# Banded attention on one core: neighbouring sums and maxima, ScalarE copies that round, and the queries' remainder at the fourth step

## The chip, the cores and the metric

One core of a Trainium2 chip runs one program. The time is the device time of one launch in microseconds, and the kernel before has 2769.32 us as the median of 3 runs (2768.60 to 2769.61). TensorE is written PE, VectorE DVE, ScalarE ACT, GpSimd POOL.

## The reference

The program computes two stacks of two layers over 1024 latent rows of width 1024, with 256 context rows beside them in the first stack. Only one part is touched: the banded attention of the first stack's odd layer (`windowed_gqa`), 16 query heads in 4 groups of 4, head size 64.

```
s_ctx  = q . kc * scale                       # all 256 context keys
s_band = q . kb * scale, -inf outside +-128   # own block of 128 and its two neighbours
p = softmax([s_ctx, s_band, sink])            # sink: one learned score per head, no value
o = p[ctx] @ vc + p[band] @ vb                # blocks: 128 queries at a time
```

## The kernel before, in words

The layer's queries are cut into 16 groups, m = 0 to 15. A group is one block of 128 queries (t = m // 2) and one of two pairs of key heads (gp = m % 2), so 8 query heads. A group walks over its tiles of 128 keys, one a step (k): two context tiles and two or three of the band. Groups 0, 1, 14 and 15 (first and last block) have 4 steps, the other twelve have 5. `gsteps` lists all steps n of all groups, `last_step[m]` is the last one of group m.

Scores are computed transposed, keys on partitions. Products are made exact enough by splitting float32 values into a rounded high part and a remainder. For the queries ACT writes the high part (`group_high_parts`, tile GQH) and DVE the remainder as "raw minus high" (`group_low_parts`, tile GQL): for gp = 1 one instruction of 128x512 (HT_R<-W,HT_R), for gp = 0 two of 128x256 (HT_R<-MIXT,HT_R and HT_R<-WORK,HT_R). Three score products of a step (the third takes GQL) and a fourth product that subtracts the row's maximum are accumulated in PSUM (line 1296).

The maximum of each query row is found one group ahead. PE makes untransposed scores of the coming group in one PSUM tile (`gqa_top`, lines 1324 to 1341: four units, and a fifth for the third band tile), and DVE takes the maximum of each unit (TENSOR_REDUCE HT<-PS, 128x1024). PE can't fill the tile again before DVE has read it. `put_top` places the units and orders them: the last unit of group m + 1 stands in the third last step of group m, and units 0 and 1 of group m + 2 in the last two steps of group m.

After the last unit comes a chain of small instructions on 8 values a row (`gqa_shift`, lines 2778 to 2788): the maximum over the units, its negative rounded into a row tile (TENSOR_SCALAR HT<-SMX), and the sink's score less the maximum (SCALAR_TENSOR_TENSOR SMX<-HT,SINK). ACT takes two exponentials of it (`gqa_sinks` of ACT), one rounded, one not. DVE subtracts the two (`gqa_sinks` of DVE, TENSOR_TENSOR HT<-SMX,HT). In the group's last step PE transposes the row tile (`gqa_rows`, line 1348, once a group), and DVE spreads it into SHIFT (TENSOR_TENSOR HT_R<-PS,HT), which the next group's scores need. In PE's order that transposition stands behind the scores of the group's last step and ahead of the value products (line 1373) of two steps earlier.

POOL sums up the weights of a group, two additions of 128x512 for each step but the first (TABL, W or WORK in the trace), each step's after ACT's exponential of that step (ACTIVATE HT<-PS 128x1024). For groups 4 to 11 it also makes two remainders of the output weights behind the additions of the third step (line 3247).

Every engine works through its instructions in program order. Nearly all instructions of DVE and ACT are recorded by one helper and so have line 169.

Of the kernel before, what the change touches and what calls it, by code (L numbers as in the profile page):

```python
# [77 lines left out]
def shape_constants():  # L78

    f = np.float32  # L80
    i = np.arange(P)
    base, stage = np.zeros((P, NCB), f), np.zeros((P, NCS_ALL), f)
    base[:, CB_ID:CB_ID + P] = np.eye(P)
    base[:, CB_CAUSAL:CB_CAUSAL + P] = i[None, :] >= i[:, None]
    stage[:, CS_WIN:CS_WIN + P] = np.where(i[None, :] >= i[:, None], 0.0, NEG)
    stage[:, CS_WIN + P:CS_WIN + 2 * P] = np.where(i[None, :] <= i[:, None], 0.0, NEG)
    stage[:, CS_STRICT:CS_STRICT + P] = np.where(i[None, :] < i[:, None], 0.0, NEG)
    row, block, half = i % 64, i[None, :] // 64, i // 64
    for n in range(4):
        stage[:, CS_FOUR + n * P:CS_FOUR + (n + 1) * P] = ((row < 12) & (row % 4 == n))[:, None]  # L90
    stage[:, CS_SINKS:CS_SINKS + P] = ((row >= 4) & (row < 12))[:, None] & (half[:, None] == block)
    stage[:, CS_ROWS:CS_ROWS + P] = (row < 4)[:, None]
    g = 1.0 - 2.0 ** (-5.0 - np.arange(RH))
    base[:, CB_QD:CB_QD + RH] = g[None, :] ** (i[:, None] + 1.0)
    base[:, CB_KD:CB_KD + RH] = g[None, :] ** (-(i[:, None] + 1.0)) * RDK ** -0.5
    for a in range(RH // 2):
        base[:, CB_GC + a] = np.where(i < 64, g[2 * a], g[2 * a + 1]) ** 128.0

    def signed(ang):
        ang = ang.astype(f).astype(np.float64)  # L100
        c, s = np.cos(ang), np.sin(ang)
        t = np.stack([np.concatenate([c, c], 1), np.concatenate([-s, s], 1)])
        return t.reshape(2, -1, P, t.shape[-1]).transpose(2, 0, 1, 3).astype(f)

    def axial(rot):
        nf = rot // 4
        inv = (f(10000.0) ** (-np.arange(nf, dtype=f) / f(nf))).astype(f)
        n = np.arange(S)
        row, col = (n // 64).astype(f), (n % 64).astype(f)
        return signed(np.concatenate([row[:, None] * inv, col[:, None] * inv], 1))  # L110

    tabs = np.zeros((4, P, TAB), f)
    mla = np.zeros((P, 2, NT, M_ROPE), f)
    mla[:, 0, :NCT] = 1.0
    mla[:, :, NCT:] = axial(M_ROPE)
    tabs[0, :, :mla[0].size] = mla.reshape(P, -1)
    tabs[1] = axial(GD).reshape(P, -1)
    inv = (f(10000.0) ** (-np.arange(32, dtype=f) / f(32))).astype(f)
    tabs[2] = signed(np.arange(S, dtype=f)[:, None] * inv[None, :]).reshape(P, -1)
    s_, t_ = i[:, None], i[None, :]  # L120
    for m in range(LEVELS):
        size = P >> m
        same = (s_ // size) == (t_ // size)
        tabs[3, :, m * P:(m + 1) * P] = same & (s_ % size < size // 2) & (t_ % size >= size // 2)
    tabs[3, :, LEVELS * P:] = np.eye(P)

    def seq_dft(n):
        r = n // P
        p, ka, kb = np.meshgrid(np.arange(P), np.arange(r), np.arange(P), indexing="ij")
        a = 2 * np.pi * ((p * (ka + r * kb)) % n) / n  # L130
        return np.stack([np.cos(a), np.sin(a)], 2) / math.sqrt(n * P)

    a = 2 * np.pi * ((i[:, None] * i[None, :]) % P) / P
    c, s = np.cos(a), np.sin(a)
    chan = np.concatenate([c, -s, s, c, -s, -c], 1)
    fft = np.concatenate([seq_dft(S).reshape(P, -1), seq_dft(CTX).reshape(P, -1), chan], 1)
    return base, stage, tabs, fft.astype(f)
# [36 lines left out]
def build(nc, A, out):  # L174

    with ExitStack() as ctx:
# [3 lines left out]
        def sem(name):  # L180
            return ctx.enter_context(nc.semaphore(name))
# [34 lines left out]
        def work(off, n):  # L216
# [61 lines left out]
                                      "sinks_ready", "rows_ready")]  # L278
        scored, weighed, valued, summed, totalled, inverted, out_taken, mixed = [
            sem(f"gqa_{n}") for n in ("scored", "weighed", "valued", "summed", "totalled", "inverted", "out_taken", "mixed")]  # L280
        gqa_const_in = sem("gqa_const_in")
        z_ready, low_ready, ln_ready, sp_ready, logs_summed, total_ready, weight_ready, decay_out, decayed_acc, block_ready, block_taken = [
            sem(f"stick_{n}") for n in ("z_ready", "low_ready", "ln_ready", "sp_ready", "logs_summed", "total_ready", "weight_ready",
                                        "decay_out", "decayed_acc", "block_ready", "block_taken")]
# [438 lines left out]
        FOUR_ROWS_R = WORK_R[:, 17920:17920 + P]  # L723
        SPARE_SUM = [work(13824, 1024), W[:, g_held, 0:1024]]
        psum_of = lambda m: (TABL[:, :] if m % 2 == 0 else SPARE_SUM[m >= 6]).rearrange("p (a c) -> p a c", a=2)
        TOP, TAIL, SINK_T, SINK_F = [SMX[:, 16 + 8 * n:24 + 8 * n] for n in range(4)]
        TOP_MAX = TOP
        TOP_OF = [HT[:, 9088 + 24 * gp:9112 + 24 * gp].rearrange("p (a i w) -> p a i w", a=2, i=4) for gp in range(2)]
        TOPS, GOUT, GSUM = PS[:, 0:1024], PS[:, 3072:3584], PS[:, 3584:4096]
        z_of = lambda n: PS[:, 1024 + 1024 * (n % 2):2048 + 1024 * (n % 2)]  # L730
# [962 lines left out]
        def _(act):  # L1693
# [320 lines left out]
            def group_high_parts(m):  # L2014
# [3 lines left out]
                    ins = f(GQH[m % 3][:, c], raw, ACT.Copy)  # L2018
                ins.then_inc(group_high, 1)

            def gqa_sinks(m):

                act.wait_ge(tops_ready, m + 1)
                f(ROWS_R[m % 2].rearrange("p (a c) -> p a c", a=2)[:, :, 4:8], heads4(SINK_T, 2), ACT.Exp)
                f(SINK_F, SINK_T, ACT.Exp).then_inc(sinks_ready, 1)

            def gqa_weigh(n):
                act.wait_ge(scored, 2 * (n + 1))
# [12 lines left out]
            nc.scalar.preload_act_table_set(EXP_AND_LN)  # L2041
            copy_unit(("gqt", NL // 2 - 1, 3), QT2[3][:, NL - 2:NL, :], 512)
            group_high_parts(1)
            gqa_sinks(0)
            slabs_done = 0
            for n in range(len(gsteps) + 2):
                m, k = group_of_step(n)
                if m is not None:
                    gqa_weigh(n)
                    if k == 0 and m + 2 < len(groups):  # L2050
                        group_high_parts(m + 2)
                    if m + 1 < len(groups) and n == last_step[m] - 1:
# [232 lines left out]
        def _(dve):  # L2285
# [492 lines left out]
            def gqa_shift(m):  # L2778

                t, gp = groups[m]  # L2780
                parts = TOP_OF[gp] if has_tail(t) else TOP_OF[gp][:, :, :, 0:3:2]
                v.tensor_reduce(heads4(TOP_MAX, 2), parts, AX_X, ALU.max)
                rows = ROWS_R[m % 2].rearrange("p (a c) -> p a c", a=2)
                if m >= 2:
                    dve.wait_ge(tops_filled, 2 * (tops_before["rows", m - 2, 0] + 1))
                v.tensor_scalar(rows[:, :, 0:4], heads4(TOP_MAX, 2), -1.0, None, ALU.mult)
                v.scalar_tensor_tensor(heads4(SINK_T, 2), ROWS[m % 2].rearrange("p (a c) -> p a c", a=2)[:, :, 0:4], G_SCALE,
                                       heads4(SINK[:, 8 * gp:8 * gp + 8], 2), ALU.mult, ALU.add).then_inc(tops_ready, 1)

            def gqa_sinks(m):  # L2790
                dve.wait_ge(sinks_ready, m + 1)
                rows = ROWS_R[m % 2].rearrange("p (a c) -> p a c", a=2)
                v.tensor_tensor(rows[:, :, 8:12], heads4(SINK_F, 2), ROWS[m % 2].rearrange("p (a c) -> p a c", a=2)[:, :, 4:8],
                                ALU.subtract).then_inc(rows_ready, 1)

            def gqa_rows(m):
                wait_tops(("rows", m, 0))
# [34 lines left out]
            for u in range(top_units(0)):  # L2832
                gqa_top(0, u)
                if u == 0:
                    for rows in ROWS:
                        v.memset(rows, 0.0)
                    for gp in range(2):
                        v.tensor_scalar(TOP_OF[gp][:, :, :, 2], heads4(SINK[:, 8 * gp:8 * gp + 8], 2), 1.0 / G_SCALE, None, ALU.mult)
            gqa_shift(0)
            group_low_parts(0)  # L2840
            dve.wait_ge(gqa_const_in, 48)
            v.tensor_copy(FOUR_ROWS_R, GPT[0][:, 0:P])
# [5 lines left out]
            for n in range(len(gsteps) + 2):  # L2848
                m, k = group_of_step(n)
                for done in after_group(n, 5):  # L2850
                    gqa_mixed(done)
                gqa_tops(n, 0)
                for done in after_group(n, 1):
                    gqa_out(done)
                if k == 1 and m + 1 < len(groups):
                    group_low_parts(m + 1)
                gqa_tops(n, 1)
                if (m, k) in ((14, 0), (15, 0)):
                    gate_diagonal(m - 14)
                if k == 3 and m in (12, 13):  # L2860
                    low_parts(2, NCT + m - 12)
# [483 lines left out]
```

## Time and profile before

| | before |
|---|---|
| median of 3 runs | 2769.32 us |
| the profiled execution | 2770.5 us |
| its span, first to last instruction | 2768.7 us |
| mean granted PE clock | 0.969 of full speed |
| PE busy | 2566.3 us (93%) |
| DVE busy | 1419.2 us (51%) |
| ACT busy | 1153.6 us (42%) |
| POOL busy | 381.1 us (14%) |

Busy times are of one profiled execution. The touched stage lies between about 1176 and 1466 us. The trace records when an instruction starts and how long it takes, including time in which it is started but held up. A row's last bracket is the idle time of its engine before it and what ended that.

### The profile page before, as it was taken

What the parts mean: (1) busy time and instruction counts of PE and PEld (TensorE: products, weight loads), DVE (VectorE), ACT (ScalarE), POOL (GpSimd) and SP (SyncE); (2) the same over time, 40 slices, a digit from 0 to 9 for tenths busy, and PEclk for the clock granted to TensorE, in tenths of its full rate; (3) what the DMA queues carried; (4) which work ended last, traced back from release to release, by engine and by line L of the source; (5) the groups of instructions that cost most, each with busy time, mean ns of one, the idle gap of its engine ahead of it and who ended that gap; (6) DMA issues with size and microseconds to landing.
All of it is one profiled execution on the core that took longest, in us unless ns stands there. A gap on an engine that the chain in (4) does not pass through costs nothing. (4 is left out here: it accounts for less than half of the span.)

```text
span 2768.7 us, 38552 instructions
## 1 busy us (share of the span) xinstructions
PE 2566.3 (93%) x14759; PEld 1979.2 (71%) x14759; DVE 1419.2 (51%) x2283; ACT 1153.6 (42%) x1977; POOL 381.1 (14%) x415
## 2 busy tenths in 40 slices
PE   4999998999999999989999999899998999999787
PEld 3778987877778878933337778786334877798776
DVE  5113265666655514666764723411777547265752
ACT  6112344454454321134443622311767647333662
POOL 1000020010020000046761000000000010004710
PEclk8999999999999999989999999999999999998889
DMA  7430010000112131110002220102000220111012
GB/s 257 174 139 24 18 33 1 1 1 1 62 54 91 47 61 46 32 37 1 1 1 91 92 78 30 59 3 76 1 1 24 84 88 31 38 47 62 1 54 76
DMA packets 87991, 139.73 MB, mean 50 GB/s; under 512 B 19513, under 2 KB 54738, under 8 KB 87682
## 3 DMA queue, kind: packets, MB, share of 16 engines
q1 hardware_dynamic: 70592, 75.90, 8.8%
q0 software_dynamic: 16976, 61.30, 6.2%
q8 instruction: 120, 1.97, 0.3%
q14 instruction: 61, 0.50, 0.1%
q10 hardware_dynamic: 242, 0.07, 0.0%
HBM read 120.47 MB, written 16.78 MB: 50 GB/s over the span
## 5 line engine op out<-in xcount | busy, mean ns | idle before, releaser
L169 ACT ACTIVATE WORK<-PS 128x512 f32<-128x512 f32 (+5 forms) x309 | 152.6, 494 | 659.2 <-PE PS L863 388.7
L863 PE MATMUL PS<-HT_R,W_R 128*128 128x512 f32 (+1 forms) x896 | 334.3, 373 | 0.0
L862 PE MATMUL PS<-WORK_R,W_R 128*128 128x512 f32 (+1 forms) x736 | 271.4, 369 | 0.0
L861 PE MATMUL PS<-WORK_R,W_R 128*128 128x512 f32 (+1 forms) x672 | 250.0, 372 | 14.4 <-DVE W_R L169 9.9
L169 ACT ACTIVATE HT<-PS 128x1024 f32<-128x1024 f32 (+6 forms) x211 | 156.0, 739 | 161.0 <-PE PS L1296 126.4
L989 PE MATMUL PS<-WORK_R,HT_R 128*128 128x512 f32 x528 | 210.3, 398 | 8.8 <-DVE W_R L169 7.5
L863 PE MATMUL PS<-W_R,WORK_R 128*128 128x256 f32 (+3 forms) x704 | 215.2, 306 | 0.0
L990 PE MATMUL PS<-WORK_R,MIXT_R 128*128 128x512 f32 x544 | 214.1, 394 | 0.0
L991 PE MATMUL PS<-W_R,HT_R 128*128 128x512 f32 x528 | 207.4, 393 | 0.0
L862 PE MATMUL PS<-W_R,HT_R 128*128 128x256 f32 (+2 forms) x688 | 206.2, 300 | 0.0
L926 PE MATMUL PS<-BASE,WORK 128*128 128x128 f32 (+1 forms) x1186 | 175.2, 283 | 25.3 <-DVE WORK L169 16.8
L863 PEld LDWEIGHTS PS<-HT_R,W_R 128*128 128x128 f32 x896 | 170.8, 191 | 29.9
L926 PEld LDWEIGHTS PS<-BASE,WORK 128*128 128x128 f32 (+1 forms) x1186 | 137.7, 143 | 54.7 <-issue 17.7
L861 PE MATMUL PS<-W_R,WORK_R 128*128 128x256 f32 (+2 forms) x560 | 169.0, 302 | 2.9 <-issue 1.4
L169 DVE TENSOR_TENSOR W_R<-W,W_R 128x1024 fp32r<-128x1024 f32 (+2 forms) x76 | 86.9, 1165 | 162.7 <-ACT W_R L169 143.5
L861 PEld LDWEIGHTS PS<-WORK_R,W_R 128*128 128x128 f32 x672 | 128.5, 191 | 43.8 <-issue 23.5
L169 DVE COPY WORK<-PS 128x512 f32<-128x512 f32 (+1 forms) x101 | 61.3, 607 | 191.7 <-PE PS L863 103.6
L862 PEld LDWEIGHTS PS<-WORK_R,W_R 128*128 128x128 f32 x736 | 140.6, 191 | 22.4 <-issue 0.5
L169 ACT ACTIVATE MIXT<-PS 128x512 f32<-128x512 f32 (+1 forms) x76 | 43.7, 575 | 262.4 <-PE PS L863 236.3
L169 ACT ACTIVATE WORK<-WORK 128x1024 f32<-128x1024 f32 (+2 forms) x88 | 78.9, 897 | 153.8 <-DVE WORK L169 149.2
L863 PEld LDWEIGHTS PS<-W_R,WORK_R 128*128 128x128 f32 x704 | 134.6, 191 | 3.9
L862 PEld LDWEIGHTS PS<-W_R,HT_R 128*128 128x128 f32 x688 | 132.1, 192 | 2.5
(328 smaller groups left out, 5587.3 us busy)
## 6 DMA issues: line engine op xcount, KB each, us to landing
MIXT<-in_w_mod POOLq DMA_DIRECT2D x8, 2048.0 KB, 8.7
x_scratch<-WORK POOLq DMA_DIRECT2D x24, 512.0 KB, 2.9
WORK<-x_scratch POOLq DMA_DIRECT2D x24, 512.0 KB, 3.6
W<-in_odd_w_in SPq DMA_DIRECT2D x12, 1024.0 KB, 5.2
W<-in_even_w_in SPq DMA_DIRECT2D x5, 2048.0 KB, 7.9
W<-in_w_mod SPq DMA_DIRECT2D x4, 2048.0 KB, 20.8
WORK<-in_x POOLq DMA_DIRECT2D x16, 512.0 KB, 8.7
W<-in_e_w_in SPq DMA_DIRECT2D x6, 1024.0 KB, 5.9
```

The source lines that it names most:

```text
L169: self.last = Signalled(self, issue(*args, **kwargs))
L861: mm(out, a[0], b_[0], start=k == 0, stop=False)
L862: mm(out, a[1], b_[0], start=False, stop=False)
L863: return mm(out, a[0], b_[1], start=False, stop=k == KT - 1)
L926: last = nc.tensor.transpose(bank[0:m, n * P:n * P + a.shape[0]], a, IDENT[0:a.shape[0], 0:a.shape[0]])
L989: mm(bank, high, wh, start=k == 0, stop=False)
L990: mm(bank, low, wh, start=False, stop=False)
L991: last = mm(bank, high, wl, start=False, stop=k == KT - 1)
```

## The change

- The small chain is written over neighbouring values. Instead of negating, scaling and adding, the row tile holds the rounded maximum in columns 0 to 3 of each half and, written once at the start, the sink's score times -1/scale in columns 16 to 19. Their sum over an innermost axis of two (a TENSOR_REDUCE) is the sink's score less the maximum, up to a factor that ACT's exponential applies. The difference of the two exponentials is a second such sum over neighbouring values, one of which ACT has negated. The constant for the fourth product changes its sign.
- The rounding of the maximum goes from DVE to ACT (`gqa_round`): a new semaphore from DVE to ACT (maximum_found) and one back (maximum_rounded). ACT has it behind its exponential of the third last step of a group; DVE's sum, a new function `gqa_sink_scores`, stands at the start of the last but one step.
- ACT had two small instructions a group and has four now (one that rounds, two exponentials, one negated copy). DVE has four small instructions before and three now, all of them TENSOR_REDUCE. At the start of the stage DVE has two more small ones, once.
- The queries' remainder (`group_low_parts(m + 1)`) moves in DVE's order from the second step (k = 1), ahead of that step's maximum, to the fourth step (k = 3), behind that step's maximum.

```diff
-    stage[:, CS_ROWS:CS_ROWS + P] = (row < 4)[:, None]
+    stage[:, CS_ROWS:CS_ROWS + P] = -1.0 * (row < 4)[:, None]
...
+            def gqa_round(m):
+                act.wait_ge(maximum_found, m + 1)
+                f(halves_of(ROWS_R[m % 2])[:, :, 0:4], heads4(TOP_MAX, 2), ACT.Copy).then_inc(maximum_rounded, 1)
...
             def gqa_sinks(m):
                 act.wait_ge(tops_ready, m + 1)
-                f(ROWS_R[m % 2].rearrange("p (a c) -> p a c", a=2)[:, :, 4:8], heads4(SINK_T, 2), ACT.Exp)
-                f(SINK_F, SINK_T, ACT.Exp).then_inc(sinks_ready, 1)
+                high = ROWS_R[m % 2].rearrange("p (a c) -> p a c", a=2)[:, :, 4:8]
+                f(high, heads4(SINK_T, 2), ACT.Exp, scale=-G_SCALE)
+                f(SINK_PAIR[:, :, :, 0], heads4(SINK_T, 2), ACT.Exp, scale=-G_SCALE)
+                f(SINK_PAIR[:, :, :, 1], halves_of(ROWS[m % 2])[:, :, 4:8], ACT.Copy, scale=-1.0).then_inc(sinks_ready, 1)
...
+                    if m + 1 < len(groups) and n == last_step[m] - 2:
+                        gqa_round(m + 1)
                     if m + 1 < len(groups) and n == last_step[m] - 1:
                         gqa_sinks(m + 1)
...
-                v.tensor_reduce(heads4(TOP_MAX, 2), parts, AX_X, ALU.max)
-                rows = ROWS_R[m % 2].rearrange("p (a c) -> p a c", a=2)
                 if m >= 2:
                     dve.wait_ge(tops_filled, 2 * (tops_before["rows", m - 2, 0] + 1))
-                v.tensor_scalar(rows[:, :, 0:4], heads4(TOP_MAX, 2), -1.0, None, ALU.mult)
-                v.scalar_tensor_tensor(heads4(SINK_T, 2), ROWS[m % 2].rearrange("p (a c) -> p a c", a=2)[:, :, 0:4], G_SCALE,
-                                       heads4(SINK[:, 8 * gp:8 * gp + 8], 2), ALU.mult, ALU.add).then_inc(tops_ready, 1)
+                v.tensor_reduce(heads4(TOP_MAX, 2), parts, AX_X, ALU.max).then_inc(maximum_found, 1)
+
+            def gqa_sink_scores(m):
+                dve.wait_ge(maximum_rounded, m + 1)
+                v.tensor_reduce(heads4(SINK_T, 2), top_and_sink(ROWS[m % 2]), AX_X, ALU.add).then_inc(tops_ready, 1)
...
-                v.tensor_tensor(rows[:, :, 8:12], heads4(SINK_F, 2), ROWS[m % 2].rearrange("p (a c) -> p a c", a=2)[:, :, 4:8],
-                                ALU.subtract).then_inc(rows_ready, 1)
+                v.tensor_reduce(halves_of(ROWS[m % 2])[:, :, 8:12], SINK_PAIR, AX_X, ALU.add).then_inc(rows_ready, 1)
...
                 for done in after_group(n, 5):
                     gqa_mixed(done)
+                if m is not None and m + 1 < len(groups) and n == last_step[m] - 1:
+                    gqa_sink_scores(m + 1)
                 gqa_tops(n, 0)
                 for done in after_group(n, 1):
                     gqa_out(done)
-                if k == 1 and m + 1 < len(groups):
+                gqa_tops(n, 1)
+                if k == 3 and m + 1 < len(groups):
                     group_low_parts(m + 1)
-                gqa_tops(n, 1)
```

DVE's rows for one group of five steps before, from the maximum of unit 1 on (128x2 is a unit's maximum, 128x8 the fifth unit's):

```order
L169 TENSOR_REDUCE HT<-PS 128x2
L169 TENSOR_TENSOR MIXT<-MIXT,PS 128x4x128
L169 TENSOR_REDUCE HT<-PS 128x2
L169 TENSOR_TENSOR MIXT<-MIXT,PS 128x4x128
L169 TENSOR_TENSOR HT_R<-W,HT_R 128x512
L169 TENSOR_REDUCE HT<-PS 128x2
L169 TENSOR_REDUCE HT<-PS 128x8
L169 TENSOR_REDUCE SMX<-HT 128x8
L169 TENSOR_SCALAR HT<-SMX 128x2x4
L169 SCALAR_TENSOR_TENSOR SMX<-HT,SINK 128x8
L169 TENSOR_REDUCE HT<-PS 128x2
L169 TENSOR_TENSOR HT<-SMX,HT 128x2x4
```

And the same stretch of DVE now, with the spreading of the rows behind it (HT_R<-PS,HT):

```order
L169 TENSOR_REDUCE HT<-PS 128x2
L169 TENSOR_TENSOR MIXT<-MIXT,PS 128x4x128
L169 TENSOR_REDUCE HT<-PS 128x2
L169 TENSOR_TENSOR MIXT<-MIXT,PS 128x4x128
L169 TENSOR_REDUCE HT<-PS 128x2
L169 TENSOR_REDUCE HT<-PS 128x8
L169 TENSOR_REDUCE SMX<-HT 128x8 x2
L169 TENSOR_REDUCE HT<-PS 128x2
L169 TENSOR_TENSOR HT_R<-W,HT_R 128x512
L169 TENSOR_REDUCE HT<-SMX 128x2x4
L169 TENSOR_TENSOR HT_R<-PS,HT 128x512
```

The remainder (HT_R<-W,HT_R) has moved from ahead of a unit's maximum to the place between the last maximum of the group and the instruction that completes the row tile for the transposition.

ACT's rows now around the small instructions of one group, where HT<-PS 128x1024 is a step's exponential and WORK_R<-W a part of the output weights that is rounded there:

```order
L169 ACTIVATE HT<-PS 128x1024
L169 ACTIVATE HT<-SMX 128x2x4
L169 ACTIVATE WORK_R<-W 128x512
L169 ACTIVATE HT<-PS 128x1024
L169 ACTIVATE HT<-SMX 128x2x4
L169 ACTIVATE SMX<-SMX 128x8
L169 ACTIVATE SMX<-HT 128x8
L169 ACTIVATE HT<-PS 128x1024
```

The first HT<-SMX is the new rounding; the weights' part and the fourth step's exponential stand behind it. PE and POOL have the same instructions in the same order as before.

## Rows read from the trace of the kernel before

**Rows 1.** Windows, groups 4 to 11: length, busy PE, PEld, DVE, ACT, POOL; clock, DMA, GB/s.
```profile
1254.60:1398.10 143.50, 133.93 (x769) 55.10 (x769) 104.17 (x108) 67.14 (x97) 102.60 (x80) 1.00 0.00 1
```

**Rows 2.** Groups by line, groups 4 to 11: busy, mean | idle before and releaser.
```profile
L1324 PE MATMUL PS<-BF 128*128 128x512 bf16 x16 | 4.8, 384 | 5.3 <-DVE HT L169 5.2
...
L1348 PE MATMUL PS<-BASE,HT 128*128 128x128 f32 x9 | 2.7, 299 | 4.3 <-DVE HT L169 3.7
```

**Rows 3.** DVE's small operations, groups 4 to 11: ns min/median/max, first and last start.
```profile
L169 DVE TENSOR_REDUCE SMX<-HT x8: 178/178/178, 1267.3 to 1393.5; 128x8 f32<-128x24 f32 x8
L169 DVE TENSOR_SCALAR HT<-SMX x8: 829/1186/1258, 1267.6 to 1393.8; 128x8 fp32r<-128x8 f32 x8
L169 DVE SCALAR_TENSOR_TENSOR SMX<-HT,SINK x8: 1186/1196/1197, 1268.4 to 1395.1; 128x8 f32<-128x8 f32 x8
L169 DVE TENSOR_TENSOR HT<-SMX,HT x8: 167/466/1145, 1271.5 to 1397.7; 128x8 fp32r<-128x8 f32 x8
L169 DVE TENSOR_TENSOR HT_R<-W,HT_R x4: 1141/1146/1149, 1261.9 to 1369.5; 128x512 fp32r<-128x512 f32 x4
...
L169 DVE TENSOR_TENSOR HT_R<-WORK,HT_R x4: 1392/1392/1392, 1280.6 to 1388.2; 128x256 fp32r<-128x256 f32 x4
```

**Rows 4.** Timeline, end of group 6: start, duration, engine, what, [idle before].
```profile
1305.43 2.62 POOL L169 TENSOR_TENSOR TABL<-TABL,HT 128x512 f32<-128x512 f32 x2
...
1305.60 1.23 DVE L169 TENSOR_REDUCE HT<-PS 128x2 f32<-128x1024 f32 x1
...
1306.00 1.20 PE L1296 MATMUL PS<-HT_R,WORK_R 64*128 64x512 f32 x8
1306.93 1.15 DVE L169 TENSOR_TENSOR HT<-SMX,HT 128x8 fp32r<-128x8 f32 x1
...
1308.23 0.30 PE L1348 MATMUL PS<-BASE,HT 128*128 128x128 f32 x1 [1.03 <-DVE HT L169]
```

**Rows 5.** Timeline, group 7.
```profile
1319.23 0.60 PE L1324 MATMUL PS<-BF 128*128 128x512 bf16 x2 [1.20 <-DVE HT L169]
...
1323.23 2.63 POOL L169 TENSOR_TENSOR W<-W,HT 128x512 f32<-128x512 f32 x2
...
1323.99 0.50 PE L1341 MATMUL PS<-WORK_R,HT_R 64*128 64x512 f32 x2
...
1324.96 1.19 PE L1296 MATMUL PS<-HT_R,WORK_R 64*128 64x512 f32 x8
...
1326.23 1.02 ACT L169 ACTIVATE HT<-PS 128x1024 f32<-128x1024 f32 x1 [1.21 <-PE PS L1296]
...
1326.28 0.30 PE L1348 MATMUL PS<-BASE,HT 128*128 128x128 f32 x1
...
1327.33 2.62 POOL L169 TENSOR_TENSOR W<-W,HT 128x512 f32<-128x512 f32 x2 [1.46 <-ACT HT L169]
```

**Rows 6.** Timeline, remainders of groups 0 and 1, ahead of POOL's first addition.
```profile
1184.47 0.43 DVE L169 TENSOR_TENSOR HT_R<-MIXT,HT_R 128x256 fp32r<-128x256 f32 x1
...
1193.40 0.69 DVE L169 TENSOR_TENSOR HT_R<-W,HT_R 128x512 fp32r<-128x512 f32 x1
```

**Rows 7.** Timeline, groups 0 and 1 (four steps).
```profile
1204.05 1.08 PE L1296 MATMUL PS<-HT_R,WORK_R 64*128 64x512 f32 x8
1204.28 1.23 DVE L169 TENSOR_REDUCE HT<-PS 128x2 f32<-128x1024 f32 x1 [0.99 <-PE PS L1341]
...
1213.26 0.29 PE L1337 MATMUL PS<-BF 128*128 128x128 bf16 x2 [1.43 <-DVE HT L169]
...
1216.58 0.30 PE L1348 MATMUL PS<-BASE,HT 128*128 128x128 f32 x1 [0.92 <-DVE HT L169]
```

**Rows 8.** Timeline, end of group 14.
```profile
1446.56 0.30 PE L1348 MATMUL PS<-BASE,HT 128*128 128x128 f32 x1 [2.49 <-DVE HT L169]
...
1448.27 1.98 PE L1383 MATMUL PS<-W,ONES 128*64 128x512 f32 x4
```

**Rows 9.** Window behind it, columns as in Rows 1.
```profile
1448.00:1450.00 2.00, 2.00 (x5) 0.29 (x4) 0.00 (x0) 0.00 (x0) 1.92 (x2) 0.53 0.00 0
```

More of the change, by code:

```diff
@@ L280, in build @@
             sem(f"gqa_{n}") for n in ("scored", "weighed", "valued", "summed", "totalled", "inverted", "out_taken", "mixed")]
-        gqa_const_in = sem("gqa_const_in")
+        gqa_const_in, maximum_found, maximum_rounded = [sem(f"gqa_{n}") for n in ("const_in", "maximum_found", "maximum_rounded")]
         z_ready, low_ready, ln_ready, sp_ready, logs_summed, total_ready, weight_ready, decay_out, decayed_acc, block_ready, block_taken = [
@@ L725, in build @@
         psum_of = lambda m: (TABL[:, :] if m % 2 == 0 else SPARE_SUM[m >= 6]).rearrange("p (a c) -> p a c", a=2)
-        TOP, TAIL, SINK_T, SINK_F = [SMX[:, 16 + 8 * n:24 + 8 * n] for n in range(4)]
-        TOP_MAX = TOP
+        TOP_MAX, SINK_PAIR, SINK_T = SMX[:, 16:24], SMX[:, 24:40].rearrange("p (a i w) -> p a i w", a=2, i=4), SMX[:, 40:48]
+        halves_of = lambda rows: rows.rearrange("p (a c) -> p a c", a=2)
+        top_and_sink = lambda rows: halves_of(rows)[:, :, 0:32].rearrange("p a (w i) -> p a i w", w=2)[:, :, 0:4, :]
         TOP_OF = [HT[:, 9088 + 24 * gp:9112 + 24 * gp].rearrange("p (a i w) -> p a i w", a=2, i=4) for gp in range(2)]
@@ L2043, in _ @@
             group_high_parts(1)
+            gqa_round(0)
             gqa_sinks(0)
@@ L2781, in gqa_shift @@
                 parts = TOP_OF[gp] if has_tail(t) else TOP_OF[gp][:, :, :, 0:3:2]
-                v.tensor_reduce(heads4(TOP_MAX, 2), parts, AX_X, ALU.max)
-                rows = ROWS_R[m % 2].rearrange("p (a c) -> p a c", a=2)
                 if m >= 2:
                     dve.wait_ge(tops_filled, 2 * (tops_before["rows", m - 2, 0] + 1))
-                v.tensor_scalar(rows[:, :, 0:4], heads4(TOP_MAX, 2), -1.0, None, ALU.mult)
-                v.scalar_tensor_tensor(heads4(SINK_T, 2), ROWS[m % 2].rearrange("p (a c) -> p a c", a=2)[:, :, 0:4], G_SCALE,
-                                       heads4(SINK[:, 8 * gp:8 * gp + 8], 2), ALU.mult, ALU.add).then_inc(tops_ready, 1)
+                v.tensor_reduce(heads4(TOP_MAX, 2), parts, AX_X, ALU.max).then_inc(maximum_found, 1)
+            def gqa_sink_scores(m):
+                dve.wait_ge(maximum_rounded, m + 1)
+                v.tensor_reduce(heads4(SINK_T, 2), top_and_sink(ROWS[m % 2]), AX_X, ALU.add).then_inc(tops_ready, 1)
             def gqa_sinks(m):
                 dve.wait_ge(sinks_ready, m + 1)
-                rows = ROWS_R[m % 2].rearrange("p (a c) -> p a c", a=2)
-                v.tensor_tensor(rows[:, :, 8:12], heads4(SINK_F, 2), ROWS[m % 2].rearrange("p (a c) -> p a c", a=2)[:, :, 4:8],
-                                ALU.subtract).then_inc(rows_ready, 1)
+                v.tensor_reduce(halves_of(ROWS[m % 2])[:, :, 8:12], SINK_PAIR, AX_X, ALU.add).then_inc(rows_ready, 1)
             def gqa_rows(m):
@@ L2837, in _ @@
                     for gp in range(2):
+                        v.tensor_scalar(halves_of(ROWS[gp])[:, :, 16:20], heads4(SINK[:, 8 * gp:8 * gp + 8], 2), -1.0 / G_SCALE, None, ALU.mult)
                         v.tensor_scalar(TOP_OF[gp][:, :, :, 2], heads4(SINK[:, 8 * gp:8 * gp + 8], 2), 1.0 / G_SCALE, None, ALU.mult)
             gqa_shift(0)
+            gqa_sink_scores(0)
             group_low_parts(0)
```

## Prediction

> **What bounds the kernel now.** I read the page first: PE is busy for 93% of the span, DVE for 51%, so an edit on DVE and ACT counts only where PE waits for them. Then the windows of the touched stage. In groups 4 to 11 PE is busy for 133.93 of 143.50 us at full clock [rows 1], so some 9.6 us of gaps are all that these eight groups can give back. Then the groups by line: PE waits 5.2 us for DVE ahead of line 1324 (the fifth unit) and 3.7 us ahead of the transposition of line 1348 [rows 2]. With both waits gone a group would last (143.5 - 8.9) / 8 = 16.8 us.
>
> The timeline says what stands behind each wait. Line 1348 waits 1.03 us at the end of even groups: DVE's last small operation starts at 1306.93 and takes 1.15 us for eight values a row, though the fastest of its kind took 0.167 [rows 3, 4]. It ends at 1308.08, at the end of POOL's additions (1305.43 + 2.62 = 1308.05) [rows 4]. The same holds for TENSOR_SCALAR (0.83 to 1.26 us), while TENSOR_REDUCE on SBUF took 0.178 us eight times of eight [rows 3]. So DVE operations of some kinds wait until the POOL instruction that is running lets go, some 0.14 us before its recorded end (1308.08 - 0.17 = 1307.91), and a reduction doesn't. Line 1324 waits 1.20 us in odd groups [rows 5], where the remainder takes two instructions ahead of a maximum, held up in the same way: 1.39 us for the second [rows 3], against 0.43 where POOL was idle [rows 6].
>
> The Trainium skill (SBUF — State Buffer, section "SBUF: two separate sides") says that VectorE and GpSimd share one pair of ports as an exclusive lock: an instruction of VectorE with two SBUF inputs and one of GpSimd never overlap there, and the one that starts first keeps it to its end. By that rule the moved remainders, which have two SBUF inputs, wait for whole POOL instructions at their new place as well, and the sum is the one below; if the two engines only shared bandwidth, they would take somewhat longer than alone and the sum would be near that of the first rival.
>
> **Small operations.** TENSOR_SCALAR and SCALAR_TENSOR_TENSOR become one reduction, and the subtraction becomes another: each about 0.18 us, never held. The first two had cover: they end at about 1305.5, when the next unit's maximum could just start (1305.60) [rows 4]. What counts is the subtraction: in the four even groups of 4 to 11 PE gets up to 1.03 us each back.
>
> The price is a trip to ACT and back. DVE's maximum goes to ACT's rounding (0.21 us as ACT's other small ones), then DVE's sum, then three small ones on ACT. Behind the rounding stand, on ACT, a part of the output weights in some groups and the exponential of the fourth step, which starts about 0.8 us later (1.4 with the weights' part). Who waits for it: POOL's additions of the fourth step, which in groups 4 to 11 are queued behind POOL's own work until 1305.43 anyway, and PE's value products, which come after the transposition. ACT ends its small ones by about 1305.2, ahead of the maximum that ends at 1306.83. So I cost the trip at 0; if that cover were gone it would be at most the 0.8 us per group. The two additional small operations at the start cost 0.4 us, and the slow operations that go in group 0 return about as much: 0.
>
> **The move, even groups (one remainder).** Taking it from the second step gives PE nothing there: no wait ahead of line 1324 in group 6. At its new place it starts when the unit's maximum ends: 1305.60 + 1.23 + 0.03 = 1306.86 [rows 4]. POOL's second addition runs until 1308.05 and lets go at 1307.91. The remainder alone takes 0.69 us [rows 6]: 1308.60. The reduction that completes the row tile: + 0.03 + 0.17 = 1308.80. PE needs 0.15 more (1308.08 to 1308.23 before): the transposition starts at 1308.95 instead of 1308.23, + 0.72 us. PE is idle from the end of the step's scores, 1307.20 [rows 4]. The wait of 1.03 us is thus not removed: it becomes 1.75.
>
> **The move, odd groups (two remainders).** The 1.20 us ahead of line 1324 go, and PE, ACT and DVE move up by them; POOL, busy without a break until 1325.86, doesn't. The unit's scores end at 1324.49 - 1.20 [rows 5], so DVE's maximum runs from 1323.36 to 1324.59. The first remainder gets on at 1325.86 - 0.14 = 1325.72 and ends at 1326.15. The second could start at 1326.18. At that moment POOL wants to add the fifth step: it started at 1327.33 before, which is 1326.13 now. A tie. If DVE wins: 1326.61, reduction 1326.81, transposition 1326.96 against 1326.28, + 0.68 us. If POOL wins, the second takes its 1.39 us: 1327.57, transposition 1327.92, + 1.64 us. The rows don't decide it, so I take the middle, + 1.16.
>
> Groups 4 to 11: 4 x 0.72 + 4 x 1.16 = + 7.5 us. Bounds: 4 x (0.72 + 1.64) = + 9.4 above. Below, POOL never in the way: even 1306.86 + 0.69 + 0.20 + 0.15 = 1307.90, - 0.33; odd 1324.62 + 0.88 + 0.20 + 0.15 = 1325.85, - 0.43; together - 3.0.
>
> **The other groups.** In a group of four steps the fourth step is the last, so the remainder now stands behind the transposition and the next group's scores need it at once. Group 0: the maximum ends at 1205.51, the remainder at 1206.2, and half of the next group's first scores (0.5 us) come after it: they end at 1206.8 instead of 1205.13 [rows 7], + 1.7. Group 1 gets back 1.43 and 0.92 us [rows 7] and loses in the same way 0.88 + the rest of the maximum, 1.8: - 0.5. Groups 2, 3, 12, 13 have no weights' part on POOL; the same walk gives about + 0.4, + 0.3, 0 and + 1.2 (the last with one more big operation of DVE ahead of the reduction), + 1.9 in all, between - 0.9 without POOL and + 3.5. Group 14: its transposition waits 2.49 us [rows 8]; without the slow operation and the remainder ahead of it, but with ACT's exponential of the third step now in the chain, it gains 0.9 and gives 0.4 back at the next scores: - 0.5. Sum + 2.6.
>
> **Sum.** + 7.5 + 2.6 = + 10.1 us. The profiled execution took 2770.5 us, 1.2 more than the median of the runs, 2769.3. So 2780.6 for a like execution, and 2779.4 us as the median. Behind the stage PE is busy again without a gap, so the delay stays.
>
> **Rivals.**
> 1. Not slower: POOL is not in the remainders' way at the fourth step. Everything is as computed but the remainders take 0.69 and 2 x 0.43 us. For it: they did so at 1184 and 1193 [rows 6]. Against: POOL's second addition covers 1306.7 to 1308.05 in each of these groups. It decides from the point where POOL's additions of the fourth step end before DVE's maximum does. - 3.0 for the eight, about - 0.1 for the others: 2769.3 - 3.1 = 2766.2 us.
> 2. Slower still by PE's clock. If POOL wins the ties, PE is idle from 1324.95 to 1327.92 in odd groups, 3.0 us. Before, the 2.49 us ahead of group 14's transposition were followed by a granted clock of 0.53, near 1.2 GHz instead of 2.4, with line 1383 at 1.98 us [rows 8, 9]; some 3 us at half rate lose an estimated 1.5. Against: waits of 1.03 and 1.20 us left the clock at 1.00 [rows 1, 4, 5]. With the upper bounds of the sum, + 9.4 + 4.2 = + 13.6, and five such drops, 7.5: 2769.3 + 21.1 = 2790.4 us. The Trainium skill (TensorE: Matmul & The Clock Gate, section "Why this matters for your kernels") warns that an idle gap of a few microseconds between bursts of matmuls sends the engine back to half rate; by it this rival would get more weight than the one drop in the trace gives it.
> 3. The move is free: the remainders end before the fourth step's maximum starts, and all waits go, 8.9 us here and some 7 in the others: 2753 us. Against: in DVE's order they stand behind that maximum.
>
> **Chances.** Forecast 0.70 (its own range 2774 to 2785), rival 1 0.11, rival 2 0.12, rival 3 0.04, the rest unknown. A measurement of this kernel can't tell 0.2%, 5.5 us, from no change. Faster by more: rival 3 and a tail of rival 1, 0.06. Within it: most of rival 1 and the lower tail of the forecast, 0.17. Slower: 0.77. The range is 2766 to 2789 us.
>
> **What would show it.** Right: the remainders sit directly ahead of a reduction HT<-SMX and take about 1.74 us (one) or 1.5 and 0.4 to 1.4 (two); waits ahead of line 1348 of 1.7 us in even and 2 to 3 us in odd groups, summing to 16 us or more over groups 4 to 11; no wait ahead of line 1324; all small operations of DVE at 0.18 us. Wrong: remainders of 0.4 to 0.7 us there, waits ahead of line 1348 under 1 us, or small operations that still take over 1 us; clock below 1.00 between 1205 and 1445 us speaks for rival 2.

## The result, and the profile after

The changed kernel takes 2804.36 us (median of 4 runs, 2803.68 to 2806.33) beside 2768.96 us of the kernel before (4 runs, 2767.89 to 2769.61): ratio 1.0131, 95% interval 1.0119 to 1.0144. It is slower, as forecast, but by 35.4 us where 10.1 were forecast, and above the range's upper end of 2789.

The profiled execution has a span of 2804.5 us and a mean granted clock of 0.962 (before 2768.7 and 0.969). The page's busy times are:

```profile
PE 2585.0 (92%) x14759; PEld 1982.2 (71%) x14759; DVE 1398.0 (50%) x2269; ACT 1163.8 (41%) x2009; POOL 380.1 (14%) x415
```

PE executes the same instructions and is busy 18.7 us longer; DVE is busy 21 us less. Nearly all of the difference lies in the touched stage: from the first matmul of the next layer to the end the span has 1303.2 us before and 1304.8 now.

Windows from one transposition to the next (length; busy PE, PEld, DVE, ACT, POOL; clock, DMA, GB/s), groups 3, 6 and 7 of the changed kernel:

```profile
1242.05:1260.51 18.46, 16.63 (x97) 6.87 (x97) 10.35 (x13) 9.20 (x16) 10.39 (x9) 1.00 0.00 1
...
1302.02:1322.08 20.06, 18.13 (x97) 7.55 (x97) 10.50 (x12) 7.53 (x13) 11.53 (x10) 0.91 0.00 1
1322.08:1343.38 21.30, 18.17 (x96) 7.58 (x97) 11.66 (x13) 8.22 (x13) 13.93 (x12) 0.92 0.00 0
```

Before, PE was busy for 133.93 / 8 = 16.7 us a group at clock 1.00 [rows 1]. Group 3 still is. Groups 6 and 7 need 18.1 and 18.2 us for the same matmuls, at 0.91 and 0.92. So two things have grown, the waits and PE's own time.

The waits, as groups of instructions in groups 4 to 11 of the changed kernel (busy, mean ns | idle before, releaser):

```profile
L169 DVE TENSOR_TENSOR HT_R<-W,HT_R 128x512 fp32r<-128x512 f32 x4 | 7.1, 1784 | 0.4
L169 DVE TENSOR_TENSOR HT_R<-MIXT,HT_R 128x256 fp32r<-128x256 f32 x4 | 6.1, 1532 | 0.4
L169 DVE TENSOR_TENSOR HT_R<-WORK,HT_R 128x256 fp32r<-128x256 f32 x4 | 5.6, 1408 | 0.1
...
L1325 PE MATMUL PS<-BF 128*128 128x512 bf16 x16 | 4.8, 384 | 0.0
L1349 PE MATMUL PS<-BASE,HT 128*128 128x128 f32 x9 | 3.0, 328 | 22.1 <-DVE HT L169 22.1
L169 DVE TENSOR_REDUCE SMX<-HT 128x8 f32<-128x24 f32 (+1 forms) x16 | 2.8, 174 | 3.2 <-ACT HT L169 2.4
...
L169 DVE TENSOR_REDUCE HT<-SMX 128x8 f32<-128x16 f32 x8 | 1.4, 170 | 0.8
```

The wait ahead of the fifth unit (line 1324, now 1325) is gone. The one ahead of the transposition (line 1348, now 1349) was 3.7 us in nine transpositions [rows 2] and is 22.1 us in the nine of this window. All small operations of DVE take 0.17 us, where they took up to 1.26 [rows 3]. The remainders take 1.78 and 1.53 + 1.41 us.

The timeline of group 7's last step shows who holds them:

```profile
1338.62 2.62 POOL L169 TENSOR_TENSOR W<-W,HT 128x512 f32<-128x512 f32 x2
1338.66 1.23 DVE L169 TENSOR_REDUCE HT<-PS 128x2 f32<-128x1024 f32 x1 [2.10 <-PE PS L1342]
1339.06 1.20 PE L1297 MATMUL PS<-HT_R,WORK_R 64*128 64x512 f32 x8
1339.99 1.53 DVE L169 TENSOR_TENSOR HT_R<-MIXT,HT_R 128x256 fp32r<-128x256 f32 x1
...
1341.42 2.67 POOL L169 TENSOR_TENSOR W<-W,HT 128x512 f32<-128x512 f32 x2 [0.18 <-ACT HT L169]
...
1341.56 1.41 DVE L169 TENSOR_TENSOR HT_R<-WORK,HT_R 128x256 fp32r<-128x256 f32 x1
1343.07 0.17 DVE L169 TENSOR_REDUCE HT<-SMX 128x8 f32<-128x16 f32 x1
1343.38 0.30 PE L1349 MATMUL PS<-BASE,HT 128*128 128x128 f32 x1 [3.13 <-DVE HT L169]
```

The first remainder ends 0.28 us after POOL's additions of the fourth step (1338.62 + 2.62 = 1341.24). POOL starts the fifth step's 0.14 us ahead of the second remainder, which then needs 1.41 instead of 0.43 us [rows 6].

And the clock in some 4 us behind each of three transpositions, those that end groups 5, 6 and 2 in order of the rows (ahead of them PE had waited 3.13, 1.93 and 1.63 us):

```profile
1302.02:1306.00 3.98, 3.98 (x17) 1.93 (x17) 1.92 (x2) 0.00 (x0) 0.71 (x1) 0.62 0.00 0
1322.08:1326.00 3.92, 3.92 (x17) 1.90 (x17) 2.14 (x3) 0.45 (x1) 1.97 (x2) 0.67 0.00 0
1242.05:1246.00 3.95, 3.95 (x23) 1.59 (x23) 2.51 (x3) 1.73 (x3) 2.09 (x2) 1.00 0.02 4
```

The granted clock falls toward half, that is from 2.4 GHz to 1.2 GHz, behind the longer two and not behind the last.

In group 7 the same eight score matmuls that took 1.09 us where the clock had stayed (see the run with filler matmuls) then take 1.91 us:

```profile
1324.18 1.91 PE L1297 MATMUL PS<-HT_R,WORK_R 64*128 64x512 f32 x8
```

The balance over the 15 stretches from the first to the last transposition: they last 260.2 us before and 296.1 after, + 35.9. PE's waits in them sum to 21.5 us before and 36.2 after, + 14.7. The other 21.2 us are PE's own time at the lower clock: 1.4 us each in groups 4 to 11 (11 in all), 2.8 in group 12 (clock 0.83), and the rest in groups 0 to 2 and 14. The 2.0 us of group 0 can't be put down to the change: its stretch took 17.47 us at clock 0.54 here and 14.92 us at 0.71 in the run with POOL's weights later, which has the same order there and the same wait of 4.1 us ahead of it. The profiled execution is also the longest of the four, 2.0 us above the median. That leaves some 19 us to the clock.

### The profile page after: what moved, and what is told of

It is laid out like the page before. It is cut to its first block and busy times, and to the rows that moved or that the text cites. A ratio compares the mean times of both kernels' runs of the same rounds, so it can differ in the third digit from the quotient of the medians.

```text
span 2804.5 us, 38602 instructions
## 1 busy us (share of the span) xinstructions
PE 2585.0 (92%) x14759; PEld 1982.2 (71%) x14759; DVE 1398.0 (50%) x2269; ACT 1163.8 (41%) x2009; POOL 380.1 (14%) x415
## 5 line engine op out<-in xcount | busy, mean ns | idle before, releaser
L169 DVE TENSOR_REDUCE HT<-PS 128x2 f32<-128x1024 f32 (+1 forms) x76 | 93.2, 1226 | 107.5 <-PE PS L1342 78.3
```

Of the source, the lines that this page charges most:

```text
L169: self.last = Signalled(self, issue(*args, **kwargs))
```

## The experiments

All are timed beside the kernel before on the same chip; its median was 2767.8 to 2771.1 us, so the ratios compare better than the times. Even and odd are groups 6 and 7; the wait is the one ahead of the transposition that ends the group.

| kernel | us, median | ratio to before, 95% | span | even: period, wait, clock | odd: period, wait, clock |
|---|---|---|---|---|---|
| before | 2768 to 2771 | | 2768.7 | 17.80, 1.03, 1.00 | 18.05, 0, 1.00 |
| changed | 2804.36 | 1.0131 (1.0119 to 1.0144) | 2804.5 | 20.06, 1.93, 0.91 | 21.30, 3.13, 0.92 |
| new operations, second step | 2765.79 | 0.9986 (0.9976 to 0.9995) | 2764.0 | 16.83, 0, 1.00 | 17.98, 0, 1.00 |
| old operations, fourth step | 2801.89 | 1.0113 (1.0098 to 1.0128) | 2799.1 | 21.31, 1.72, 0.85 | 20.63, 4.00, 0.97 |
| new operations, third step | 2752.76 | 0.9932 (0.9917 to 0.9947) | 2751.6 | 16.68, 0, 1.00 | 16.68, 0, 1.00 |
| old operations, third step | 2755.90 | 0.9945 (0.9928 to 0.9962) | 2753.3 | 17.80, 1.14, 1.00 | 16.72, 0, 1.00 |
| new, fourth step, ahead of the maximum | 2760.26 | 0.9960 (0.9944 to 0.9976) | 2751.3 | 16.68, 0, 1.00 | 17.24, 0.61, 1.00 |
| changed, POOL's weights later | 2786.64 | 1.0063 (1.0046 to 1.0080) | 2784.9 | 17.59, 0.92, 1.00 | 17.73, 1.10, 1.00 |
| changed, filler matmuls | 2793.45 | 1.0086 (1.0070 to 1.0101) | 2787.4 | 18.58, 0.55, 1.00 | 19.76, 1.73, 1.00 |
| new, third step, + 1.23 us on DVE | 2769.20 | 1.0003 (0.9993 to 1.0012) | 2769.4 | 17.94, 1.31, 1.00 | 17.94, 1.31, 1.00 |
| the same, + 1.95 us | 2804.30 | 1.0128 (1.0110 to 1.0147) | 2801.7 | 20.22, 2.04, 0.92 | 20.15, 2.04, 0.92 |
| the same, + 2.5 us | 2811.35 | 1.0154 (1.0135 to 1.0172) | 2811.4 | 20.79, 2.57, 0.92 | 20.80, 2.57, 0.92 |

### Which part makes the loss

The small operations alone (`group_low_parts` back at the second step):

```diff
-                gqa_tops(n, 1)
-                if k == 3 and m + 1 < len(groups):
+                if k == 1 and m + 1 < len(groups):
                     group_low_parts(m + 1)
+                gqa_tops(n, 1)
```

> The new small operations and the rounding on ACT, with the queries' remainders back at the second step. Theory (the move made the loss, the small operations are a gain): the waits ahead of the transposition go (4 x 1.03 us in groups 4 to 11, about 0.9 us in group 1 and 1 us in group 14), the 1.20 us ahead of the fifth unit in odd groups stay: 2769 - 6 = 2763 us, clock 1.00 in groups 2 to 13. Rival (the trip to ACT and back makes the loss): 2790 to 2804 us, with waits ahead of the transposition as in the changed kernel.

Measured 2765.79 us, a small gain, 0.14%; its interval ends at 0.9995, just short of no change. The even groups' wait ahead of the transposition (0.65 us in group 4, 1.03 in the other three) is gone; the odd groups' 1.20 ahead of the fifth unit stays. Less than the 6 us came, in part because group 14's chain waits 2.80 instead of 2.49 us, with ACT's exponential now inside it.

The move alone, on the kernel before:

```diff
-                if k == 1 and m + 1 < len(groups):
-                    group_low_parts(m + 1)
                 gqa_tops(n, 1)
+                if k == 3 and m + 1 < len(groups):
+                    group_low_parts(m + 1)
```

> The kernel before with only the move to the fourth step. Theory: the whole loss is here, and a little more than in the changed kernel, since the subtraction ahead of the transposition can be held by POOL as well: 2804 to 2812 us, waits ahead of the transposition of 1.9 us or more in even and 3.1 us or more in odd groups, clock near 0.92 in the groups from the fifth on. Rival (the trip to ACT makes the loss): 2766 to 2775 us.

Measured 2801.89 us: the whole loss is in the move, within the intervals (1.0113 against 1.0131). The waits are 1.72 and 4.00 us in most pairs of groups. The end of an odd group, with two remainders and then the addition of 128x8, all three held by POOL:

```profile
1292.33 2.63 POOL L169 TENSOR_TENSOR WORK<-WORK,HT 128x512 f32<-128x512 f32 x2
...
1293.83 1.42 DVE L169 TENSOR_TENSOR HT_R<-MIXT,HT_R 128x256 fp32r<-128x256 f32 x1
...
1295.14 2.66 POOL L169 TENSOR_TENSOR WORK<-WORK,HT 128x512 f32<-128x512 f32 x2 [0.18 <-ACT HT L169]
...
1295.28 1.40 DVE L169 TENSOR_TENSOR HT_R<-WORK,HT_R 128x256 fp32r<-128x256 f32 x1
1296.79 1.04 DVE L169 TENSOR_TENSOR HT<-SMX,HT 128x8 fp32r<-128x8 f32 x1
...
1297.97 0.45 PE L1348 MATMUL PS<-BASE,HT 128*128 128x128 f32 x1 [4.00 <-DVE HT L169]
```

The clock doesn't fall as regularly as in the changed kernel (0.99 to 0.85), and the time came out 2 us below the lower end expected.

### Other places for the remainders

At the third step ahead of its maximum, with the new operations and with the old:

```diff
-                gqa_tops(n, 1)
-                if k == 3 and m + 1 < len(groups):
+                if k == 2 and m + 1 < len(groups):
                     group_low_parts(m + 1)
+                gqa_tops(n, 1)
```

> The changed kernel with the remainders at the third step, ahead of its maximum, where DVE has 2.5 us without work and POOL is between two steps' additions. Theory: the remainders end before the fifth unit's scores do, all waits ahead of lines 1325 and 1349 go in groups 4 to 11 (8.9 us) and some 5 to 7 us elsewhere: 2753 to 2756 us, clock 1.00. Rival (a remainder costs wherever it stands behind POOL): waits ahead of the fifth unit of 1 us in odd groups, 2763 us, no better than the small operations alone.

> The kernel before with only the remainders at the third step. Theory: the odd groups' 1.20 us ahead of the fifth unit go, the even groups' 1.03 us ahead of the transposition stay, and groups 1, 2 and 13 gain 1.4, 0.85 and 1.2 us: 2769 - 9 = 2760 us. Rival: the remainders now push the slow TENSOR_SCALAR and SCALAR_TENSOR_TENSOR onto PE's path, 2769 us or more.

2752.76 and 2755.90 us. With the new operations no wait is left in groups 3 to 11, and a group lasts 16.68 us, the 16.8 that the prediction had for a group without waits. The second remainder takes 0.43 us there in place of 1.39. The kernel with the old operations came out 4 us below the 2760 expected. A part of that is scatter ahead of the stage: the first transposition stands at 1181.2 us in its profiled execution and at 1186.8 with the new operations. Between the first and the last transposition the old operations take 249.8 us and the new ones 243.0, against 260.2 before. A second measurement gave 2753.29 us (0.9944, 0.9931 to 0.9956) for the same kernel, against this expectation:

> The new small operations with the remainders at the third step once more, beside the run before on one chip: 2752 to 2753 us, 0.994 of the kernel before.

In groups 4 to 11 of this kernel:

```profile
L1325 PE MATMUL PS<-BF 128*128 128x512 bf16 x16 | 4.8, 384 | 0.0
L169 DVE TENSOR_TENSOR HT_R<-W,HT_R 128x512 fp32r<-128x512 f32 x4 | 4.3, 1076 | 0.4
L169 DVE TENSOR_TENSOR HT_R<-MIXT,HT_R 128x256 fp32r<-128x256 f32 x4 | 3.6, 900 | 0.4
L1349 PE MATMUL PS<-BASE,HT 128*128 128x128 f32 x9 | 2.7, 299 | 0.5
L169 DVE TENSOR_TENSOR HT_R<-WORK,HT_R 128x256 fp32r<-128x256 f32 x4 | 1.7, 426 | 0.1
```

The fourth step, but ahead of that step's maximum instead of behind it:

```diff
-                gqa_tops(n, 1)
                 if k == 3 and m + 1 < len(groups):
                     group_low_parts(m + 1)
+                gqa_tops(n, 1)
```

> The changed kernel with the remainders still in the fourth step but ahead of its maximum. DVE waits 2.1 us there for that unit's scores. Theory: a single remainder (held by POOL's own work, 1.8 us at most) still fits; two (0.9 + 1.4 us) end 0.5 us late and delay the maximum and the transposition by as much: even groups 16.8 us, odd ones 17.3 us; 2756 to 2762 us, clock 1.00. Rival (the step is what matters, not the side of the maximum): 2790 us or more.

Even groups 16.68, odd ones 17.24 us, as expected to a tenth. The same step costs 44 us more or less depending on the side of one maximum (medians 2804.36 against 2760.26). Its three runs scatter from 2753 to 2761 us, and the profiled one is the shortest, so its rank among the good ones is open.

### POOL's part

POOL's remainders of the output weights behind the fifth step's additions:

```diff
-                        if k == 2 and done < 2 * KT and m >= 4:
+                        if k == 4 and done < 2 * KT and m >= 4:
```

> The changed kernel with POOL's two remainders of the output weights (groups 4 to 11) behind the fifth step's additions instead of behind the third's. POOL then begins the fourth step's additions when ACT's exponential ends, about 1 us earlier. Theory (the wait is for POOL's instruction): the waits ahead of the transposition shrink to 0.9 to 1.2 us in even and 1.3 to 2.0 in odd groups 4 to 11, the clock stays at 1.00 where the wait is below about 1.6 us: 12 to 20 us below the changed kernel, 2785 to 2792. Rival (the remainders are long by themselves at this place): waits stay 1.93 and 3.13 us, 2804 us.

2786.64 us. The timeline of its group 6's end, where POOL does nothing between 1315.07 (1312.44 + 2.63) and 1316.30:

```profile
1312.44 2.63 POOL L169 TENSOR_TENSOR TABL<-TABL,HT 128x512 f32<-128x512 f32 x2 [1.39 <-ACT HT L169]
...
1314.86 0.76 DVE L169 TENSOR_TENSOR HT_R<-W,HT_R 128x512 fp32r<-128x512 f32 x1
...
1316.05 0.30 PE L1349 MATMUL PS<-BASE,HT 128*128 128x128 f32 x1 [0.92 <-DVE HT L169]
```

In groups 6 and 7 the waits fall to 0.92 and 1.10 us and the periods by 2.5 and 3.6 us; the remainder of group 6's end takes 0.76 instead of 1.78 us, so POOL's instruction had cost it 1.02 us. In groups 4, 5 and 8 to 11 ACT also rounds weights ahead of the fourth step's exponential (in group 8 for 0.63 us from 1346.63), POOL's additions start late again (there at 1348.76, and the remainder takes 1.75 us), and the waits are 1.6 to 1.9 us. That part of the expectation missed.

### The clock

Six matmuls ahead of each transposition, whose results nobody reads:

```diff
                 open_tops(("rows", m, 0))
+                if m:
+                    for _ in range(6):
+                        mm(heads4(TOPS[:, 512:1024]), WIN_BF[:, 0:P], ID_BF.unsqueeze(1).to_broadcast([P, 4, P]), start=True, stop=True,
+                           skip_group_check=True)
                 pe.wait_ge(rows_ready, m + 1)
```

> The changed kernel with six matmuls of 512 columns, whose results nobody reads, on PE ahead of each transposition but the first, where PE waits anyway. Theory (what the prediction lacked is the clock, lost in nearly every group): the transpositions come at the same offset, the granted clock stays at or near 1.00, groups 4 to 11 last 18.7 (even) and 19.9 us (odd) instead of 20.1 and 21.3: 11 to 15 us less, 2789 to 2793 us. Rival (the clock costs nothing, the periods are long because of DVE and ACT): 2804 us or more.

2793.45 us (4 runs, 2789 to 2798), 11 us less than the changed kernel for 6 x 15 = 90 matmuls more. The timeline of group 6's end, with line 1353 as the transposition:

```profile
1309.40 1.19 PE L1297 MATMUL PS<-HT_R,WORK_R 64*128 64x512 f32 x8
1310.52 1.47 PE L1350 MATMUL PS<-BF 128*128 128x512 bf16 x6
1312.54 0.30 PE L1353 MATMUL PS<-BASE,HT 128*128 128x128 f32 x1 [0.55 <-DVE HT L169]
1312.77 1.08 PE L1378 MATMUL PS<-HT,WORK 128*64 128x512 f32 x4
...
1314.33 1.09 PE L1297 MATMUL PS<-HT_R,WORK_R 64*128 64x512 f32 x8
```

The transposition comes 2.0 us behind the scores as in the changed kernel, and the scores that follow take 1.09 us, against 1.91 there. In seven of the groups 4 to 11 the clock is 1.00 and the periods are 18.6 and 19.8 us. Group 8 has 0.92 behind a wait of 1.73, for which I have no cause.

DVE held up by itself, in the kernel with the remainders at the third step. Its results go where nobody reads them, and neither a remainder nor an operand read from SBUF is in it:

```diff
                     elif what == "rows":
+                        v.tensor_reduce(SMX[:, 0:2], halves8(TOPS), AX_X, ALU.max)
+                        v.tensor_reduce(SMX[:, 2:4], halves8(TOPS[:, 0:512]), AX_X, ALU.max)
                         gqa_sinks(m)
```

> The kernel with the new small operations and the remainders at the third step (no wait of PE in groups 3 to 11), and DVE held up in front of each group's last small reduction by two maxima over PSUM that nobody reads (128x1024 and 128x512, 1.23 + 0.7 us). It makes PE wait some 1.8 us ahead of every transposition with no remainder and no POOL instruction in it. Theory (a wait of PE of this size is enough to drop the clock, whatever causes it): 12 groups x 1.8 us of waits and a clock of 0.91 to 0.92 in most of groups 3 to 12, 1.4 us each: 2753 + 22 + 11 to 17 = 2786 to 2792 us, periods of 18.5 us in groups where the clock stays and 19.9 where it drops. Rival (the clock falls because of what POOL and DVE do in the changed kernel): 2775 us, clock 1.00 throughout.

2804.30 us (two runs). The wait is 2.04 us at the end of groups 2 to 11 (2.39 in group 8) and the clock 0.92 in eight of the nine groups 3 to 11; the kernel is 51 us slower than the one it is built on, with 29 us of added waits in it (33.0 against 3.8). Groups 4 and 12 of the same kernel kept their clock, which gives the price directly: groups 4 and 5 have the same wait ahead of them and at their end. Their windows:

```profile
1264.08:1282.74 18.66, 16.63 (x96) 6.86 (x97) 11.80 (x14) 9.21 (x16) 12.59 (x11) 1.00 0.01 2
1282.74:1302.99 20.25, 18.21 (x96) 7.41 (x97) 11.96 (x15) 9.02 (x15) 12.60 (x11) 0.92 0.00 1
```

The drop costs 20.25 - 18.66 = 1.6 us, all of it in PE's busy time (18.21 against 16.63). The wait that ends group 5:

```profile
1300.62 1.95 DVE L169 TENSOR_REDUCE SMX<-PS 128x2 f32<-128x1024 f32 x2
...
1302.99 0.30 PE L1349 MATMUL PS<-BASE,HT 128*128 128x128 f32 x1 [2.04 <-DVE HT L169]
```

The time is 12 us above the expectation: the drops were more, and in groups 2 and 14 deeper (0.81).

With two full maxima (the second line reads all of TOPS):

> As the run before, with two maxima of 128x1024 (2 x 1.25 us), a wait of some 2.3 us ahead of every transposition. Theory: the clock falls in every group from 3 to 12, periods of 16.7 + 2.3 + 1.4 = 20.4 us: 2753 + 29 + 18 = 2800 us. Rival (POOL and DVE together drop the clock): 2782 us, clock 1.00 throughout.

2811.35 us (two runs), the clock at 0.86 to 0.92 in every group from 3 to 12. The periods are mostly 20.7 to 20.8, where 20.4 was expected; two are 21.1 and 22.0.

With the first of the two lines alone:

> The kernel with the remainders at the third step and one maximum over PSUM of 128x1024 (1.23 us) that nobody reads in front of each group's last small reduction. With two of them (1.95 us together) PE waited 2.04 us ahead of the transpositions, so here about 1.3 us. Theory (the price of a wait has a step in it: below some size the clock stays): clock 1.00 in groups 3 to 12, periods of 16.7 + 1.3 = 18.0 us, 2753 + 14 x 1.3 = 2771 us. Rival (the clock's price is in proportion to the wait): 0.95 in each group, periods of 18.9 us, 2783 us.

2769.20 us: wait 1.31 and period 17.94 in groups 4 to 11, and clock 1.00 in all groups from 1 to 13. One of them:

```profile
1291.33:1309.27 17.94, 16.63 (x96) 6.86 (x97) 11.11 (x13) 7.96 (x14) 12.61 (x11) 1.00 0.00 1
```

From 1.31 to 2.04 us of waiting the kernel loses 35 us, of which 15 x 0.73 = 11 are the waiting. The rival, a price in proportion, falls: it wanted a clock of 0.95 and 2783 us at a wait of 1.31.

### An attempt to gain more

The kernel with the remainders at the third step, with DVE's large remainder of the next layer (MIXT_R, 128x1024) one step later in groups 12 and 13:

```diff
-                if k == 3 and m in (12, 13):
+                if k == 4 and m in (12, 13):
```

> The new small operations with the remainders at the third step, and DVE's two large remainders of the next layer (MIXT_R, groups 12 and 13) a step later, in the fifth, behind the transposition. The wait of 1.38 us ahead of group 13's transposition goes and no other comes: 1.4 us less than the same kernel without it, 2751 us. Rival: the large operation then holds up the spreading of the rows or a maximum in the next group, no gain or a loss of up to 1.2 us.

2753.88 us (0.9944, 0.9930 to 0.9957): no gain. The 1.38 us ahead of group 13's transposition go, but the operation, held by POOL for 2.10 us in all, now delays a maximum (PE waits 1.16 us), and its twin in group 14 pushes the diagonal behind it into POOL's additions (0.63 and 1.43 us). The rival was right.

## Why the prediction was right and wrong

- **The small operations** were right: reductions at 0.17 us in every group, the trip through ACT without cost in groups of five steps, a small gain when alone (0.9986).
- **The place of the move** was right, and the lock with it: one remainder 1.78 us (forecast 1.74), PE's wait in even groups 1.93 (forecast 1.75). Most of the 0.18 us between forecast and measurement are the starts behind one another: 0.10 us from the maximum to the remainder and 0.10 to the reduction, where I took 0.03 each.
- **The tie** went to POOL, in all four odd groups: 3.13 us of waiting, against 2.97 for this branch. The middle was no estimate of anything that could happen; the groups repeat, so the tie falls the same way each time. This step cost 4 x 0.48 = 1.9 us.
- **The other groups** were undersized: groups 0 and 1 lose 2.01 and 1.86 us at the next scores, as forecast with 1.7 and 1.8, but group 2 grew by 0.78 us (1.63 for 0.85), group 3 by 0.62 (1.82 for 1.20) and group 13 by 1.61 (4.19 for 1.20 and 1.38), above the + 0.4, + 0.3 and + 1.2 of the walk. At the end of group 13 the first remainder got through, while the second and the large operation (1.23 us alone) met POOL:

```profile
1461.21 0.42 DVE L169 TENSOR_TENSOR HT_R<-MIXT,HT_R 128x256 fp32r<-128x256 f32 x1
...
1461.67 1.37 DVE L169 TENSOR_TENSOR HT_R<-WORK,HT_R 128x256 fp32r<-128x256 f32 x1
...
1463.15 2.10 DVE L169 TENSOR_TENSOR MIXT_R<-MIXT,HT_R 128x1024 fp32r<-128x1024 f32 x1
1465.35 0.17 DVE L169 TENSOR_REDUCE HT<-SMX 128x8 f32<-128x16 f32 x1
1465.67 0.45 PE L1349 MATMUL PS<-BASE,HT 128*128 128x128 f32 x1 [4.19 <-DVE HT L169]
```

Group 14's wait shrank by 0.72 us (1.77 for 2.49), but group 15's first scores wait 1.50 us, where the walk had 0.4. The waits of the 15 stretches together grew by 14.7 us, where the sum had 10.1 and its upper end 13.6. By the waits alone the kernel would take 2769 + 15 = 2784 us, inside the range.

- **The step that failed is the clock.** The prediction set its price to 0 in the sum and kept it for a rival of 0.12, in five odd groups only, on the ground that waits of 1.03 and 1.20 us had left the clock at 1.00. But its own sum had waits of 1.75 us in even groups and 2 to 3 in odd ones, and for the latter the nearest row of before was the 2.49 us of group 14, with its drop [rows 8, 9]; 1.75 us lay between that row and the 1.20. The trace shows some 19 us from the clock: it fell behind every wait of 1.82 us and more in the changed kernel, at the end of even groups too. Rival 2's time, 2790, was short by the drops behind the even groups' waits, by those in groups 1, 2 and 14, and by a deeper one in group 12.
- The Trainium skill (TensorE: Matmul & The Clock Gate, section "Why this matters for your kernels") pointed there: it tells to avoid idle gaps of PE between bursts of matmuls, since they bring the lower rate back. The traces agree with its direction; the waits behind which the clock fell here, 1.8 to 2.6 us among them, are shorter than the gaps it names, and the measurement decides.
- The Trainium skill's rule on the shared ports (SBUF — State Buffer, section "SBUF: two separate sides"), by which the engine that starts first keeps them, held for the remainders: 0.43 us of work took 1.41 when POOL had started 0.14 us earlier. The small reductions from SBUF to SBUF took 0.17 to 0.18 us, all 48 of the changed kernel.

## What to carry to other kernels

Moving work out of one gap of an engine is only worth it if the new place has a gap too: look at the side of the wait that PE depends on, here behind or ahead of one maximum, 44 us apart. When a change lengthens PE's waits from about 1 to about 2 us, price the clock as well, by the nearest row with a wait of that size, not by the shorter ones. A tie between two engines that repeats in a loop goes one way in all its turns: forecast one branch.

## What the runs showed of the hardware

- The granted clock stayed at 1.00 behind repeated waits of 1.31 us, and fell behind most of those of 2.04 and all of 2.57. Between lie mixed cases: with POOL's weights later, waits of 1.60, 1.82 and 1.91 us had no drop and others of 1.63 and 1.82 had one; in the changed kernel 1.63 had none and 1.82 had one; among the filler matmuls 1.73 had one and three others of 1.73 had none. Most drops cost 1.4 to 1.6 us of PE's time in a group; some cost more (19.6 instead of 16.6 us of busy time in group 6 of the old operations at the fourth step, behind a wait of 4.00).
- Six matmuls in each wait, whose results nobody reads, gave back 11 us: the kernel got faster by more instructions on its busiest engine.
- POOL's additions of 1.31 us held a DVE operation with two SBUF operands up to about 1.1 us, whatever its size: eight values a row in 1.19 us [rows 3], 128x256 in 1.41.
